# Attention rows in the order 3, 0, 4, 1, 5, 2, 6, 7 instead of 0 to 7, with three masks added late by POOL

## The reference

```
s = einsum(q, k) * scale + cum_q - cum_k
s = where(k_pos <= q_pos, s, MASK_VALUE)
p = softmax(s)
attn = p @ v
h = h + concat(headRMS(attn), headRMS(conv)) @ w_out
u2 = RMSNorm(h)                 # then: router, top-1 group, top-2 experts, SwiGLU experts
```

## Time and profile before

| | us |
|---|---|
| median of 3 runs | 1261.03 (1259.76 to 1261.53) |
| the profiled execution: its own time | 1260.95 |
| its span in the trace | 1259.2 |
| attention, from the first scores to the last row's | 379.13 to 574.28 |
| the same with the last row | to about 612 |

### The profile page before, as it was taken

How to read it: one execution, slowest core, us unless ns; L and a number is a source line. 1 busy time by engine, 2 the same in 40 slices (tenths; PEclk the granted TensorE clock), 3 DMA queues, 4 the chain that set the end, 5 groups by cost and what they waited for, 6 DMA issues and landing times.

```text
span 1259.2 us, 18115 instructions
## 1 busy us (share of the span) xinstructions
PE 1129.4 (90%) x6677; PEld 853.6 (68%) x6677; DVE 631.9 (50%) x909; ACT 533.5 (42%) x804; POOL 216.3 (17%) x256
## 2 busy tenths in 40 slices
PE   6999999999998999998887999999899999989960
PEld 6999988899995666666666886655565555555530
DVE  6422233334335566665577875555545444445526
ACT  7302141143335454454345864554544544444520
POOL 4000001132000111101123112222222212222210
PEclk9999999999999999999998999999999999999985
DMA  9420015333004333222178999999999999999869
GB/s 264 101 68 1 1 48 186 134 108 130 1 1 134 89 97 85 68 80 72 69 302 321 362 370 406 418 424 403 404 391 375 408 389 397 409 389 394 354 245 361
DMA packets 66249, 291.53 MB, mean 232 GB/s; under 512 B 10696, under 2 KB 36328, under 8 KB 53648
## 3 DMA queue, kind: packets, MB, share of 16 engines
q1 hardware_dynamic: 48176, 243.38, 50.8%
q0 software_dynamic: 16720, 42.65, 9.1%
q10 hardware_dynamic: 1296, 4.72, 0.9%
HBM read 270.62 MB, written 37.92 MB: 245 GB/s over the span
## 4 chain that ended last, share of the span: by engine, by line
PE 59%; DMA 21%; DVE 7%; ACT 6%; issue 6%; SPq 1%; DVEq 0%; ACTq 0%; POOLq 0%
DMA wu<-in_w_up 15%; PE ps L1025 9%; PE ps L1027 9%; PE ps L1026 9%; PE ps L1389 4%; DMA wd<-in_w_down 3%; PE ps L1341 3%; PE ps L1343 3%; PE ps L1342 3%; PE ps L1152 3%; PE ps L1120 2%; PE ps L1134 2%; DMA y<-expert_rows 2%; PE ps L1330 2%; DVE probs L2094 1%
## 5 line engine op out<-in xcount | busy, mean ns | idle before, releaser
L2146 DVE TENSOR_TENSOR wu_low<-wu,wu_high 128x2048 fp32r<-128x2048 f32 x36 | 81.1, 2286 | 57.1 <-ACT wu_high L1684 57.1
L1355 PE MATMUL ps<-wg,xa 128*64 128x512 f32 x224 | 102.1, 598 | 0.0
L1355 PE MATMUL ps<-wu,xa 128*64 128x512 f32 x224 | 102.1, 598 | 0.0
L1684 ACT ACTIVATE wd_high<-wd 128x2048 fp32r<-128x2048 f32 x36 | 66.8, 1905 | 81.0 <-DMA wd<-in_w_down 79.2
L2146 DVE TENSOR_TENSOR wd_low<-wd,wd_high 128x2048 fp32r<-128x2048 f32 x36 | 81.2, 2287 | 36.3 <-ACT wd_high L1684 36.0
L1684 ACT ACTIVATE wu_high<-wu 128x2048 fp32r<-128x2048 f32 x36 | 66.9, 1907 | 70.0 <-DMA wu<-in_w_up 70.0
L2146 DVE TENSOR_TENSOR wg_low<-wg,wg_high 128x2048 fp32r<-128x2048 f32 x36 | 81.0, 2288 | 21.0 <-ACT wg_high L1684 21.0
L2249 DVE TENSOR_TENSOR hid<-sil,ps 128x512 f32<-128x512 f32 x18 | 12.3, 685 | 130.3 <-PE ps L1343 130.3
L1684 ACT ACTIVATE wg_high<-wg 128x2048 fp32r<-128x2048 f32 x36 | 66.9, 1908 | 25.3 <-DMA wg<-in_w_gate 24.2
L965 POOL DMA_INDIRECT expert_rows<-yb,idxs x32 | 45.5, 1420 | 164.4 <-ACT yb L1733 126.6
L1025 PE MATMUL ps<-uh,w_high 128*128 128x342 f32 (+1 forms) x208 | 71.4, 343 | 0.0
(11 more groups left out here) (388 smaller groups left out, 2941.9 us busy)
## 6 DMA issues: line engine op xcount, KB each, us to landing
wg<-in_w_gate SPq DMA_DIRECT2D x32, 2048.0 KB, 17.0
wu<-in_w_up SPq DMA_DIRECT2D x32, 2048.0 KB, 19.1
wd<-in_w_down SPq DMA_DIRECT2D x32, 2048.0 KB, 20.3
u_rows<-u POOLq DMA_DIRECT2D x16, 512.0 KB, 6.3
y<-expert_rows SPq DMA_DIRECT2D x16, 512.0 KB, 12.1
raw_c<-in_w_in SPq DMA_DIRECT2D x5, 1024.0 KB, 5.3
xin<-in_x SPq DMA_DIRECT2D x8, 512.0 KB, 10.0
zx<-in_x POOLq DMA_DIRECT2D x4, 1024.0 KB, 7.1
```

Source lines behind the costliest of these rows:

```text
L1355: last = mm(ps[HALF * n:HALF * (n + 1), 7, :], xa[:, k, :], raw[m][:, 1, k, :], start=(k == 0), stop=(k == KT - 1))
L1684: A(flat_half(wh[m][:, :, :], n), flat_half(raw_kf(m, s), n), ACT.Copy).then_inc(w_high[m], 1)
L2146: return V.tensor_tensor(flat_half(wl[m][:, s, :, :], n), flat_half(raw_kf(m, s), n), flat_half(wh[m][:, :, :], n).bitcast(F32), ALU.subtr ...
```

## The change

Row `ROWS[i]` takes the place of row i, with `ROWS = (3, 0, 4, 1, 5, 2, 6, 7)`. Units 0 to 3 are row 3, units 4 to 7 row 0, and so on. Rows 6 and 7 stay where they were. The extras stay in the same units as before, and belong to the row that is there. Masks: before attention POOL adds them to the blocks of rows 3 to 7 alone. Those of rows 0, 1 and 2 it adds when the longer row ahead has been taken, since that row needs the block whole. The table `BEFORE_TURNS` is emptied, and only units 0 and 1 keep their three unread products: 26 of 32 are gone there. Everything that was indexed with i in DRAM, in `expid`, `sloti` and `gates` is indexed with the row.

```diff
-BEFORE_TURNS = {("U0", 0): 8, ("U1", 0): 2, ("U0", 1): 4}
+BEFORE_TURNS = {}
+ROWS = (3, 0, 4, 1, 5, 2, 6, 7)
+LATE = [i for i in range(1, NT) if ROWS[i] < ROWS[i - 1]]
 def width(i):
-    return META + P * (i + 1)
+    return META + P * (ROWS[i] + 1)
 def turns(u):
-    blocks = [(a, j) for a in range(2) for j in range(u // PAIRS + 2)]
+    blocks = [(a, j) for a in range(2) for j in range(ROWS[u // PAIRS] + 2)]
...
-                        at = META + P * i
+                        at = META + P * ROWS[i]
                         for h in (2 * c, 2 * c + 1):
                             sp.dma_start(ck(h)[:, at:at + P], ck_rows[h, at:at + P].partition_broadcast(P)
...
-                    own = half_ck[:, h, META:].rearrange("p (t k) -> p t k", k=P)
-                    nc.gpsimd.tensor_tensor(own, own, maskf[:, :].unsqueeze(1).broadcast_to([P, NT, P]),
+                    own = half_ck[:, h, META:].rearrange("p (t k) -> p t k", k=P)[:, ROWS[0]:, :]
+                    nc.gpsimd.tensor_tensor(own, own, maskf[:, :].unsqueeze(1).broadcast_to([P, NT - ROWS[0], P]),
...
+            def mask_row(i):
+                at = META + P * ROWS[i]
+                for c in range(PAIRS):
+                    pool.wait_ge(scores_taken, 2 * (PAIRS * (i - 1) + c) + 2)
+                    for h in (2 * c, 2 * c + 1):
+                        own = ck(h)[:, at:at + P]
+                        nc.gpsimd.tensor_tensor(own, own, maskf[:, :], ALU.add).then_inc(ck_masked[c // 2], 1)
...
+            mask_row(LATE[0])
             for i in range(NT):
...
+                if i + 3 in LATE:
+                    mask_row(i + 3)
...
-                n = i + 2
+                n = ROWS[i] + 2
...
-                if u < first_step(0):
+                if u < 2:
                     stream(7, 3)
...
+                if i in LATE:
+                    dve.wait_ge(ck_masked[c // 2], H // 2 * (LATE.index(i) + 1) + 2 * (c % 2 + 1))
```

More of the change, by code:

```diff
@@ L718, in _ @@
                     sp.wait_ge(u2_ready, i)
-                sp.dma_start(h1b[:, :], dram_part[P * i:P * (i + 1), :]).then_inc(xr_in, 16)
+                sp.dma_start(h1b[:, :], dram_part[P * ROWS[i]:P * (ROWS[i] + 1), :]).then_inc(xr_in, 16)
             sp.wait_ge(pv_done, UNITS)
@@ L892, in _ @@
                 wait_x_used(pool, ("W1", i))
-                pool.dma_start(dram_h1[P * i:P * (i + 1), :], h1b[:, :]).then_inc(h1_out, 16)
+                pool.dma_start(dram_h1[P * r:P * (r + 1), :], h1b[:, :]).then_inc(h1_out, 16)
                 if i == 1:
@@ L1119, in scores @@
                         half_rows = slice(HD * a, HD * (a + 1))
-                        last = mm(big[:, o:o + n], qT[half_rows, c, P * i:P * (i + 1)],
+                        last = mm(big[:, o:o + n], qT[half_rows, c, P * ROWS[i]:P * (ROWS[i] + 1)],
                                   kT[half_rows, c, b:b + n], start=True, stop=True)
@@ L2012, in extra @@
                     then(V.max_index(top8i[:, 1, :], top8[:, 1, :], rk2[:, 1, :]))
-                    then(V.tensor_copy(expid[:, :, i], top8i[:, 1, 0:2]))
+                    r = ROWS[i]
+                    then(V.tensor_copy(expid[:, :, r], top8i[:, 1, 0:2]))
                     for k in range(2):
-                        then(V.tensor_scalar(one[:, k, :], iota128[:, 0:NE], expid[:, k, i:i + 1], None, ALU.is_equal))
+                        then(V.tensor_scalar(one[:, k, :], iota128[:, 0:NE], expid[:, k, r:r + 1], None, ALU.is_equal))
                     then(V.tensor_tensor(both[:, i, :], one[:, 0, :], one[:, 1, :], ALU.add))
@@ L2072, in extra @@
                     then(V.tensor_reduce(jblk[:, :], over7[:, :, :], AX.X, ALU.add))
-                    then(V.scalar_tensor_tensor(rank[:, :], rank[:, :], float(TABC), expid[:, :, i], ALU.mult, ALU.add))
-                    V.scalar_tensor_tensor(sloti[:, :, i], jblk[:, :], float(NE - P * TABC), rank[:, :],
+                    then(V.scalar_tensor_tensor(rank[:, :], rank[:, :], float(TABC), expid[:, :, ROWS[i]], ALU.mult,
+                                                ALU.add))
+                    V.scalar_tensor_tensor(sloti[:, :, ROWS[i]], jblk[:, :], float(NE - P * TABC), rank[:, :],
                                            ALU.mult, ALU.add).then_inc(slot_ready, 1)
@@ L2078, in extra @@
                     then(V.scalar_tensor_tensor(gden[:, :], gratio[:, :], 1.0, gsum[:, :], ALU.add, ALU.mult))
-                    then(V.reciprocal(gates[:, 0, i:i + 1], gden[:, :]))
-                    V.tensor_tensor(gates[:, 1, i:i + 1], gates[:, 0, i:i + 1], gratio[:, :], ALU.mult)
+                    r = ROWS[i]
+                    then(V.reciprocal(gates[:, 0, r:r + 1], gden[:, :]))
+                    V.tensor_tensor(gates[:, 1, r:r + 1], gates[:, 0, r:r + 1], gratio[:, :], ALU.mult)
             def take_scores(u, a):
```

8 lines of the change are left out of this document (5 added, 3 removed).

## The result

| | before | changed |
|---|---|---|
| median of 7 runs, us | 1261.03 | 1267.92 (1261.8 to 1269.42 but for one) |
| ratio, 95% interval | | 1.004 (1.0022 to 1.0057) |
| the same kernel again, median of 11 runs | 1261.24 | 1264.25 (1261.93 to 1272.1) |
| ratio of that, 95% interval | | 1.0037 (1.0018 to 1.0055) |

The change costs about 5 us (1261.03 x 0.004), between 2.8 and 7.2. I had forecast 1.1. A ratio here is taken over all executions of both kernels, and is not that of the two medians beside it. The profiled execution of the first measurement was disturbed (2249 us, its matmuls 1.7 to 1.9 times as long) and is left out of the ratio, so the profile after is that of the second measurement, whose own time was 1263.07.

A forecast was written before the change was run, and what follows sets the result against it. PE was busy 90% of the span, with attention's waits set by DVE and ACT chains. Terms 5.9 + 0 - 3.7 - 0.5 - 0.6 = +1.1 us on 1260.95 gave 1262.05, median 1262.1, range 1258.2 to 1265.6.

The forecast's parts named there:

- the price of 0 and -0.6: Unread products before U0 fill a wait, removal 0; the two before U1 lie on the path, removal -0.6 us.
- PE's clock falls: Rival: waits in units 6 and 7 halve PE's clock; one fall gives 1263.6, two 1265.1; chance 0.27.
- Units 0 to 6: Start of attention, four units of row 3 and three of row 0: 26.5 us against 20.56, +5.9.
- Unit 7: Row 0 instead of row 1: chain length stays 10.37 us, idle before W0 grows to about 2.4; cost 0.
- Row 1's step: Row 1's step with all extras replaces row 3's 29.81: 26.1 us, -3.7 (bounds -5.3 and -3.2).
- The sum for attention: All terms in attention, 5.9 + 0 - 3.7 - 0.5 - 0.6: +1.1 us, passed to the end one to one.
- the shorter left-overs of rows 4, 5 and 6: Second unit of each step computes the row ahead's last products with v; over all steps two rows less, -0.5 us.
- the waiting saved at the start: Side comparison at the start, 26.5 for 20.85 of work against 20.56 for 12.6: 1.9 us of saved waiting.
- The rival that the waits are covered: Long rows' left-over work fills short rows' waits: 1257.6, faster; row 7's scores below 192.5 would show it; chance 0.13.
- The masks: 24 late additions on POOL, 0.31 us each: cost 0, bound 2.5; rival that they stop DVE: 1264.6, chance 0.05.

The follow-up runs named there:

- the run with held-back masks: Kernel before, its four low masks ahead of attention held back until the first half's last query product is made: 1261.66 against 1261.67, ratio 0.9996.
- with its waits filled: Changed kernel plus unread products ahead of W0 (unit 7), ahead of U0 and between U0 and U1 (units 8, 16): 1259.31, ratio 0.9989 against before.
- threefold masks: Changed kernel with each of the 24 late masks added three times, one after the other: 1266.71, ratio 1.0048 against the kernel before.

## Why the prediction was wrong

**The step that failed** is the price of 0 and -0.6 for taking out the unread products, with no term for the clock in the sum; the clock stood in the rival "PE's clock falls" alone, and that was priced too low. Its mechanism is what happened; I gave it 0.27, with one or two falls at 1.5 us each. Three falls covered 13.7 us, the longest of them 6.8, and cost 1.6, 1.4 and 2.5, in all 5.5 us of the profiled execution. Taking them away gave 5 to 6 us (medians 1264.25 to 1259.31, ratios 1.0037 to 0.9989). Two mistakes lie in it. I had found in the earlier trace rows that the eight products before U0 "fill a wait", and priced their removal at 0 because PE idles in their place; what they held up was the clock. The old order without them falls four times. And I looked for close waits in units 6 and 7 only, when a pair of waits, before U0 and before U1, stands in each step where a short row's left-over is all that there is to bridge them: units 8, 16 and 24, of which the first two fell. My argument against it, that 1.71 us of idle had left the clock at 1.00, was of one wait with unread products in the units ahead, and of one execution: the same wait with the same products stood ahead of a fall in the run with held-back masks (403.8).

**Units 0 to 6**: 26.64 for 26.5. Unit by unit 2.66, 4.32, 3.97, 3.97, 4.42, 2.28, 5.02 against 2.7, 4.4, 3.9, 3.9, 3.2, 2.7, 5.7. The first four hold. Unit 4 is 1.2 longer, units 5 and 6 are 0.4 and 0.7 shorter: the sum is right partly by chance.

**Unit 7**: forecast 10.37, measured 11.92, and 10.29 with its waits filled. The idle time before W0 is 2.11, as forecast (over 2). Before the product with v in unit 6 it is 1.39, not over 2. U0 follows W1 as forecast: scores of unit 8 at 414.88, U0 at 418.89, 4.0 us.

**Row 1's step** with its left-over: forecast 27.2 (by the prediction's own terms 26.1 + 3 x 0.27, which is 26.9), measured 25.85. I took 1.4 for what the smaller row saves, between 0.9 and 3.0; 2.5 came true (28.09 - 0.57 + 0.81 - 25.85). **The sum for attention**: 0.8 measured with the waits filled, 1.1 forecast. That it comes out so near is partly luck: row 1's step gave 1.1 us more than its terms, and the shorter left-overs of rows 4, 5 and 6 gave 1.6 and not 2.4 (steps of 31.3, 33.7 and 39.8 us, which were 31.8, 34.2 and 40.3). One comparison in the prediction is off, though nothing in the sum uses it: 26.5 less 20.85 is 5.65 and 20.56 less 12.6 is 7.96, so that the waiting saved at the start was 2.3 by these figures, not 1.9.

**The rival that the waits are covered** is refuted by those idle times and by row 7's scores, at 199.9 after the first and not below 192.5.

**The masks**: late ones make no unit of attention longer, as forecast, though one takes 0.456 and not 0.31. The early ones I priced at 0, for "DVE is not seen slowed by them". Those rows are POOL's own durations, and the one that is slowed is DVE. The shorter masks gave back 1.9 us ahead of attention. I had even cited the Trainium skill's rule for this pair of engines and applied it to the late masks only. Without this gain the change would have cost more.

**What is open**: how the 5 us are shared in all the executions that have no trace (in the one profiled it is 1.6 for W0's wait and 3.9 for the U0-U1 pairs, but 1261.12 and 1259.31 overlap in their intervals, and falls come and go, as the one in unit 15 does); where the threefold masks' 1.4 us in the ratio come from, if they are real; and whether held-back masks help the old order and hurt the new one, for both pairs of intervals overlap.

## What to carry to other kernels

A product that nobody reads is worth nothing by its own time and may be worth a fall of the clock: before taking it away, ask what else PE does in the few us around it, and if it lies on a chain of handovers, move it into a wait instead of removing it. When work is reordered, list each place where two waits come to stand close to each other, in every step and not only where the first one is found. One trace at full clock does not show that such a wait is safe: the next execution may fall there. Where POOL runs a long element-wise instruction, read the rows of DVE beside it and compare with the same DVE instruction elsewhere; POOL's own row doesn't show what it costs.

## What the runs showed of the hardware

- The longest idle time of PE ahead of the three falls of the change was 2.11 us. One fall came at 420.7, between waits of 1.68 and 1.18 us with 0.63 us of transposes among them (418.89 to 421.06). A fall can begin in a wait (420.7) or under work (407.1, 478.7), and its price falls on the work that comes then: 2 of 2 us busy at 0.50.
- Falls differ from one execution of a kernel to the next: the changed kernel had its falls at 407.1, 420.7 and 478.7, and the one with threefold masks, the same on PE, at 408.3, 421.9 and 480.0; and row 6's fall came in the profiled execution of before and not in that of the change. With the same instructions in attention and the same 1.71 us of idle, the clock fell in unit 7 in the run with held-back masks and not in the kernel before. The change, with more falls, spreads a little more (1261.93 to 1272.1, before 1257.25 to 1264.75).
- The Trainium skill's page TensorE: Matmul & The Clock Gate, part 1, calls the throttled state the default, which activity releases. The trace agrees: fillers that compute nothing of use took three falls away (ratio 1.0037 to 0.9989).
- A DVE `tensor_tensor` with two inputs in SBUF that starts while POOL's mask runs ends only some 0.3 us behind that mask: 0.42 us becomes 2.37 beside a mask of 1024 columns and 1.57 beside one of 640. One that started 0.03 us ahead of the mask took 0.43. The other way round POOL's instruction grows: a late mask of 0.456 us took 1.37 when it met DVE's `wol` of 1.22, which had started 0.16 us earlier.
